# One planned step of a hybrid decoder: both tiles of a group ranked in one stage, the sample's keys loaded at once and its queries spread by TensorE, and the order of all engines planned anew

## The reference, cut to what matters

```python
def block(hc):                                   # 128 tokens
    q = (hc @ w_q).reshape(PEER_CHUNK, PEER_HEADS, 2, PEER_QDIM // 2)
    sc = jnp.einsum('chpd,hpkd->chpk', q, sub_keys)
    s1, i1 = lax.top_k(sc[:, :, 0], 16)
    s2, i2 = lax.top_k(sc[:, :, 1], 16)
    cand = s1[..., :, None] + s2[..., None, :]   # 256 sums a head
    top_s, pos = lax.top_k(cand, 16)             # 16 experts a head, 8 heads
    gate = jax.nn.softmax(top_s, axis=-1)
    act = jax.nn.gelu(einsum('cd,chkd->chk', hc, u[eid]))
    return einsum('chk,chkd->cd', gate * act, v[eid])
```

## Time and profile before

| | us |
|---|---|
| median of 3 executions | 3265.84 (3263.42 to 3266.49) |
| the profiled execution | 3275.52 |
| its span, first to last instruction | 3273.7 |

### The profile page before, as it was taken

The page is one execution under the profiler, slowest core; times in us unless marked ns, Lnnn a source line. Parts: engine busy times, 40 slices in busy tenths (PEclk is TensorE's granted clock), DMA queues, the critical chain, the costliest instruction groups (busy, mean ns, idle before and its releaser), DMA issues.

```text
span 3273.7 us, 38234 instructions
## 1 busy us (share of the span) xinstructions
PE 2734.6 (84%) x9152; PEld 1497.6 (46%) x9152; DVE 2532.3 (77%) x6009; ACT 1827.8 (56%) x5820; POOL 1411.1 (43%) x1044
## 2 busy tenths in 40 slices
PE   7777798889989889989988888579878778878886
PEld 4444354445545545554445545234444334444442
DVE  1288687888788998878888887656989987777775
ACT  1245544678555668755556677344555555555554
POOL 0034232444333444434344454223444456666663
PEclk9888999999999999989999999799999999999998
DMA  9999899999999999999999999988999999999997
GB/s 335 357 387 397 338 392 419 385 377 409 399 391 417 388 398 400 387 365 422 390 361 396 383 395 409 351 300 346 373 372 391 386 403 418 421 420 421 416 418 295
DMA packets 191372, 1262.55 MB, mean 386 GB/s; under 512 B 24849, under 2 KB 32873, under 8 KB 46737
## 3 DMA queue, kind: packets, MB, share of 16 engines
q0 software_dynamic: 149760, 1086.39, 82.5%
q1 hardware_dynamic: 41384, 173.70, 14.2%
HBM read 1251.24 MB, written 43.37 MB: 395 GB/s over the span
## 4 chain that ended last, share of the span: by engine, by line
DMA 28%; DVE 26%; PE 24%; issue 7%; ACT 6%; DVEq 5%; POOL 2%; SPq 1%; ACTq 1%; POOLq 0%
DMA uv_ring<-in_peer_uv,idx 25%; DVE uv_ring L2467 10%; PE acc L1775 9%; DVE accs L2474 5%; PE pS L1530 4%; PE pS L1657 3%; PE pA L1680 2%; POOL uv_ring L1471 1%; ACT bent L2072 1%; ACT wv L2075 1%; ACT diag L1845 1%; DVE onehot L2326 1%; DVE onehot L2329 1%; PE acc L1530 1%; PE pS L1584 1%
## 5 line engine op out<-in xcount | busy, mean ns | idle before, releaser
L1471 POOL DMA_INDIRECT uv_ring<-in_peer_uv,idx x1024 | 1394.5, 1362 | 1816.5 <-PE acc L1775 1352.5
L1775 PE MATMUL acc<-uv_ring,diag 128*128 128x512 f32 x2460 | 1242.9, 638 | 378.5 <-ACT diag L1845 373.3
L2467 DVE SCALAR_TENSOR_TENSOR uv_ring<-uv_ring,hb 128x1024 f32<-128x1024 f32 x1032 | 1240.2, 1221 | 280.0 <-DMA uv_ring<-in_peer_uv,idx 253.5
L1775 PEld LDWEIGHTS acc<-uv_ring,diag 128*128 128x128 f32 x2460 | 454.0, 198 | 943.2 <-ACT diag L1845 525.7
L2068 ACT ACTIVATE cube<-dots 128x1 f32<-128x1 f32 x1032 | 205.8, 199 | 874.5 <-DVE uv_ring L2467 866.2
L2474 DVE SCALAR_TENSOR_TENSOR accs<-uv_ring,wv,accs 128x1024 f32<-128x1024 f32 x409 | 523.4, 1280 | 44.0 <-ACT wv L2075 42.1
L1789 PE MATMUL acc<-maskB,zeros 128*96 128x256 f32 x2162 | 520.8, 384 | 0.0
L1789 PEld LDWEIGHTS acc<-maskB,zeros 128*96 128x96 f32 x2162 | 353.4, 165 | 205.5 <-issue 118.1
L2072 ACT ACTIVATE bent<-dots,cube 128x1 f32<-128x1 f32 x1032 | 399.1, 387 | 74.1 <-issue 2.8
L1845 ACT ACTIVATE diag<-diag,wv 128x128 f32<-128x128 f32 x615 | 247.0, 402 | 50.8 <-issue 1.4
L2075 ACT ACTIVATE wv<-bent,dots 128x1 f32<-128x1 f32 x615 | 238.0, 387 | 43.9 <-issue 1.4
(11 more groups left out here) (279 smaller groups left out, 2225.2 us busy)
## 6 DMA issues: line engine op xcount, KB each, us to landing
wbuf<-in_w_q SPq DMA_DIRECT2D x40, 1024.0 KB
out_dil_s<-in_cache_dil SPq DMA_DIRECT2D x8, 4092.0 KB
wbuf<-in_w_in SPq DMA_DIRECT2D x26, 1024.0 KB
wbuf<-in_w_out SPq DMA_DIRECT2D x20, 1024.0 KB
uv_ring<-in_peer_uv,idx POOLq DMA_INDIRECT x1024
uv_ring<-in_w_in SPq DMA_DIRECT2D x6, 1024.0 KB, 16.3
keysT<-in_keys SPq DMA_DIRECT2D x40, 128.0 KB
T<-in_xT_all SPq DMA_DIRECT2D x8, 512.0 KB, 15.1
```

The source lines that it names most:

```text
L1471: pool.indirect_dma_start(uv_ring[:, entry % RING, :], None, peer_uv, bass.IndirectOffsetOnAxis(rows, 0))\
L1775: m = pe.matmul(acc[0:R, side * 512:(side + 1) * 512], w, uv_ring[:, entry % RING, D + side * 512:D + (side + 1) * 512], start=first, stop ...
L2467: dve.scalar_tensor_tensor(row, row, GELU_C, h, ALU.mult, ALU.mult, accum_out=dots[:, e % RING:e % RING + 1]).then_inc(u_dot, 1)
```

## The change

- A group's two tiles are ranked together: one `r0` and one `r1` for both, so that `top16` runs its five steps over four (or two) parts with one drain ahead of each step. The second tile's sums go into a new buffer, `cand2`, inside `onehot`. The numbers of `max`, `max_index` and `match_replace` are the same as before.
- The sample's queries are no longer spread by DMA. A new stage `sq` on PE (`sample_queries`) multiplies a column of the unit matrix, broadcast, with the eight new query rows, twice 512 columns, into `pS` for even and `pT` for odd tokens; the products read them there. `sq` of token r waits for the products of token r - 2.
- The space of the queries holds keys: each of the 8 tokens has its own buffer `s_kv`, its keys are loaded for all eight right after `sin`'s loads with no wait between, and its values come into the same buffer once its own products are done.
- The planner's numbers: `SPREAD` 1.8 to 2.4, `DMA8` 2.62 to 2.5, the sample's transfers all at `sin` (12.0) and 1.5 for the values of each token, 10 us (`NEW_ROWS`) until the new rows are back, 6 + 3r us until the keys of token r are there and 14 us for values.

```diff
     out = [("sin", 0, 0, 0, 0.0, 2.0)]
+    out += [("sq", 0, 0, 1, 0.9, 0.0)]
     for r in range(NS):
-        out += [("smul", r, 0, 2, 0.0, 2.6), ("smul", r, 1, 0, 0.0, 1.6)]
+        out += [("sq", r + 1, 0, 1, 0.9, 0.0)] if r + 1 < NS else []
+        out += [("smul", r, 0, 1, 0.0, 2.6), ("smul", r, 1, 0, 0.0, 1.6)]
...
-        for t in tiles:
-            out += [("r0", g, h, 0, 0.0, 3.3, t), ("r1", g, h, 0, 0.0, 2.2, t)]
+        out += [("r0", g, h, 0, 0.0, 3.3, tiles), ("r1", g, h, 0, 0.0, 2.2, tiles)]
...
+    if kind in ("r0", "r1"):
+        return (("DVE", {"r0": (3.23, 5.56), "r1": (2.75, 4.43)}[kind][len(s[6]) - 1]),)
...
-SPREAD = 1.8
+SPREAD = 2.4
...
-DMA8 = 2.62
+DMA8 = 2.5
 POOL = 1.4
 FETCH = 12.0
-S_SETS = 4
+NEW_ROWS = 10.0
...
-        if s[0] in ("smul", "spv"):
-            return 1.9
+        if s[0] == "sin":
+            return 12.0
+        if s[0] == "smul" and s[2] == 1:
+            return 1.5
...
+        if BASE[n][0] == "sin" or BASE[n][0] == "sq" and BASE[n][1] < 2:
+            ready += NEW_ROWS
         if BASE[n][0] in ("smul", "spv") and BASE[n][2] == 0:
 
             r = BASE[n][1]
-            if BASE[n][0] == "spv":
-                m = AT["smul", S_SETS + r // 2, 1]
-            else:
-                m = AT["sin", 0, 0] if r < S_SETS else AT["smul", r - S_SETS, 1]
+            m, late = (AT["smul", r, 1], FETCH + 2.0) if BASE[n][0] == "spv" else (AT["sin", 0, 0], 6.0 + 3.0 * r)
             end = self.part_end.get((m, 0))
             if end is None:
                 return None
-            ready = max(ready, end + FETCH)
+            ready = max(ready, end + late)
...
+        cand2 = onehot[:, 1, :, :].rearrange("p a b -> p (a b)")[:, 0:136]
...
-        s_sets = [(KTBf if i < 2 else VBf)[:, 2048 * (i % 2):2048 * (i % 2) + 2048] for i in range(S_SETS)]
-        s_k = [x[:, 0:1024].rearrange("p (s n) -> p s n", s=2) for x in s_sets]
-        s_q = [x[:, 1024:2048] for x in s_sets]
-        s_v = [s_sets[r // 2][:, 1024 * (r % 2):1024 * (r % 2) + 1024].rearrange("p (s n) -> p s n", s=2)
-               for r in range(NS)]
+        s_kv = [(KTBf if r < 4 else VBf)[:, 1024 * (r % 4):1024 * (r % 4) + 1024].rearrange("p (s n) -> p s n", s=2)
+                for r in range(NS)]
...
+        s_kA = [o_all[:, 256 + P * r:384 + P * r] if r < 6 else rest[:, 2752 + P * (r - 6):2880 + P * (r - 6)]
+                for r in range(NS)]
...
+        s_q = [pS, pT]
...
             def sample_keys(r):
-                i = r % S_SETS
-                if r >= S_SETS:
-                    sp.wait_ge(s_mul, r - S_SETS + 1)
-                for dst, src in cache_rows(s_k[i], r, 0):
-                    sp.dma_start(dst, src).then_inc(sk_in[i], 16)
-                sp.dma_start(s_kA[i], cache_swa[r:r + 1, :].rearrange("r (s n) -> (r s) n", n=256)[:, 0:P])\
-                  .then_inc(sk_in[i], 16)
-                sp.dma_start(s_q[i][:, 0:512], zS_scr[r:r + 1, QA:KVA].broadcast_to([P, 512])).then_inc(sk_in[i], 16)
-                sp.dma_start(s_q[i][:, 512:1024], zS_scr[r:r + 1, QB:KB].broadcast_to([P, 512])).then_inc(sk_in[i], 16)
+                for dst, src in cache_rows(s_kv[r], r, 0):
+                    sp.dma_start(dst, src).then_inc(sk_in[r], 16)
+                sp.dma_start(s_kA[r], cache_swa[r:r + 1, :].rearrange("r (s n) -> (r s) n", n=256)[:, 0:P])\
+                  .then_inc(sk_in[r], 16)
...
-                        for r in range(S_SETS):
+                        for r in range(NS):
                             sample_keys(r)
                         sample_masks()
                     elif s[0] == "smul" and s[2] == 1:
-                        if s[1] + S_SETS < NS:
-                            sample_keys(s[1] + S_SETS)
-                        else:
-                            for r in range(2):
-                                sample_values(2 * (s[1] - S_SETS) + r)
+                        sample_values(s[1])
...
-                sp.wait_ge(s_mul, S_SETS + r // 2 + 1)
+                sp.wait_ge(s_mul, r + 1)
...
+            def sample_queries(r):
+
+                if r == 0:
+                    pe.wait_ge(snew_in, 64)
+                    need(pe, a_max, seen["sm"])
+                if r == 1:
+                    need(pe, n_T, seen["ng"])
+                if r > 1:
+                    pe.wait_ge(s_mul, r - 1)
+                for side in range(2):
+                    m = pe.matmul(s_q[r % 2][:, 512 * side:512 * side + 512], idn[0:8, r:r + 1].broadcast_to([8, P]),
+                                  s_newq[:, side, :], start=True, stop=True)
+                m.then_inc(sq_mm, 1)
...
-            def rank_halves(g, h, t):
-                u = PLACE_IN_GROUP[t]
+            def rank_halves(g, h, tiles):
                 dve.wait_ge(k_ev, 16 * g + 2 * h + 2)
                 parts = [(sc[:, (16 * g + 2 * h + half) % SC_SLOTS, u * P:(u + 1) * P], topv[:, u, half, :],
-                          topi[:, u, half, :]) for half in range(2)]
-                m = top16(parts)
-                if t == prompt_of(GROUPS[g])[-1]:
-                    m.then_inc(r_top, 1)
-
-            def rank_sums(u, R):
-
-
-                first, second = topv[0:R, u, 0, :], topv[0:R, u, 1, :]
-                D_()
-                dve.tensor_tensor(cand[0:R, 0:128].rearrange("p (a b) -> p a b", b=8),
-                                  first.unsqueeze(2).broadcast_to([R, TOPK, 8]),
-                                  second[:, 0:8].unsqueeze(1).broadcast_to([R, TOPK, 8]), ALU.add)
-                dve.tensor_scalar(cand[0:R, 128:136], second[:, 8:16], first[:, 0:1], None, ALU.add)
-                top16([(cand[0:R, :], candv[0:R, u, :], candp[0:R, u, :])])
-                return dve.tensor_scalar(gsub[0:R, u, :], candv[0:R, u, :], candv[0:R, u, 0:1], None, ALU.subtract)
+                          topi[:, u, half, :]) for u in range(len(tiles)) for half in range(2)]
+                top16(parts).then_inc(r_top, 1)
+
+            def rank_sums(us, R):
+
+
+                D_()
+                cands = {u: (cand if i == 0 else cand2)[0:R, :] for i, u in enumerate(us)}
+                for u in us:
+                    first, second = topv[0:R, u, 0, :], topv[0:R, u, 1, :]
+                    dve.tensor_tensor(cands[u][:, 0:128].rearrange("p (a b) -> p a b", b=8),
+                                      first.unsqueeze(2).broadcast_to([R, TOPK, 8]),
+                                      second[:, 0:8].unsqueeze(1).broadcast_to([R, TOPK, 8]), ALU.add)
+                    dve.tensor_scalar(cands[u][:, 128:136], second[:, 8:16], first[:, 0:1], None, ALU.add)
+                top16([(cands[u], candv[0:R, u, :], candp[0:R, u, :]) for u in us])
+                for u in us:
+                    m = dve.tensor_scalar(gsub[0:R, u, :], candv[0:R, u, :], candv[0:R, u, 0:1], None, ALU.subtract)
+                return m
...
                 if part == 0:
-                    dve.wait_ge(sk_in[r % S_SETS], 96 * (r // S_SETS + 1))
-                    dot_heads(s_sc[:, 0:2, 8 * r:8 * r + 8], s_k[r % S_SETS].unsqueeze(2),
-                              s_q[r % S_SETS][:, 512:1024].unsqueeze(1).unsqueeze(1).broadcast_to([P, 2, 1, 512]),
+                    dve.wait_ge(sk_in[r], 64)
+                    dve.wait_ge(sq_mm, r + 1)
+                    dot_heads(s_sc[:, 0:2, 8 * r:8 * r + 8], s_kv[r].unsqueeze(2),
+                              s_q[r % 2][:, 512:1024].unsqueeze(1).unsqueeze(1).broadcast_to([P, 2, 1, 512]),
                               1024, P, (2, 1, 2))
```

30 lines of the change are left out of this document (18 added, 12 removed).

## The result

The changed kernel takes 3243.08 us, the median of 5 executions (3241.09 to 3247.91), and the kernel before 3266.49 us beside it (3263.42 to 3274.04). The ratio is 0.9917, 95% interval 0.9895 to 0.9938: 23 us less by the medians, 20 to 34 us by the interval. The profiled execution took 3242.59 us, its span is 3241.0 us. The forecast was 3223 us, so 20 us too good; as a ratio it is 0.987, outside the interval.

What follows compares the result with a forecast made beforehand. The prediction took the DMA gathers as the bound, so gains come from unmoved bytes or a dry ring. Its terms 13 + 17 + 13 = 43 us gave 3232 for the profiled execution, 3223 us as median; range 3190 to 3272.

Steps and rivals of the forecast that it cites:

- Bytes, 13 us: Sample's attention: dropping 16 query spreads, 4.19 MB, saves 13 us, since DMA is nearly full there.
- Rival D: Small transfers slow the gathers beside them, so removing the spreads gains more: 3192 us; chance 0.06.
- The sample's waits, 17 us between 0 and 34: Sample's attention and output projection: fewer waits for loads fill DMA's dry spells, worth at most 34 us; half taken, 17.
- The signs for it: From `sin` to output projection: 370 GB/s or more, no slice under 200, DVE's load waits under 10 us.
- The ranking, 13 us: Ranking two tiles at once saves DVE 1.7 us a head, 41 us in all; 13 counted as time.
- The sign for it: The stretch of the last ranking should run at 385 GB/s or more.
- The order, 0 within 19 us: New lists over the 1850 us ahead of the sample: no effect, bounds 19 us either way.
- Rival C: The new lists lose elsewhere: the 1850 us run at 382 GB/s, 47 us longer, giving 3270 us; chance 0.11.
- The other sign of being wrong: The prediction would be wrong if POOL waits for `idx`, a ranking, after the start.
- The spread on PE, 0: Sample's queries: 16 products take 17 us of PE beside DMA, costing nothing; queries read from PSUM add nothing.
- Rival B: Sample's attention: PE and DVE hold each other up behind late loads, waits of 90 us, 3296 us; chance 0.11.
- Rival A: Only the bytes count; waits move to a crowd of loads and ranking was hidden: 3253 us; chance 0.17.

Runs made afterwards that it cites:

- x2: The changed kernel with its lists kept and the 16 query spreads issued again as loads nobody waits for; 3246.14 us, 0.9932.
- x6: The kernel before with the sample's part of the change alone, old planner numbers, ranking one tile a stage; 3233.70 us, 0.9890.
- x7: The kernel before with the sample's part and the new planner numbers, ranking one tile a stage; 3234.00 us, 0.9893.
- x4: The kernel before, planned with the new SPREAD 2.4 and DMA8 2.5 and otherwise untouched; 3274.47 us, 1.0024.
- x3: The changed kernel planned with the old SPREAD 1.8 and DMA8 2.62; 3257.61 us, 0.9963.
- x5: The kernel before with the merged ranking stages alone, planned anew with the old numbers; 3287.35 us, 1.0054.
- x9: The changed kernel, with its planner expecting a token's values 54 us after its products instead of 14; 3241.37 us, 0.9922.
- x11: x7 with the eight 64 KB loads of near values issued early, right behind the masks; 3234.21 us, 0.9897.
- x10: x7 with every list kept, but both tiles' first two ranking stages done at once at the second tile's place; 3280.45 us, 1.0039.

## Why the prediction was right, and where it was not

The direction and the main reason, the sample's part, held; the sum, 43 us, was 20 too high. That 3243 lies in the range says little, since 3190 to 3272 reached past no change. The sample's part was forecast at 30 us and measured at 30 to 40, and that is in part luck: its two terms were wrong in opposite directions.

- **Bytes, 13 us.** As bytes it is right: 169.50 MB on q1, 1258.25 MB in all, as forecast. As time it is 3 to 5 us (x2), give or take as much again. The step that failed is "DMA is nearly full there, so I take 13 us as saved": the stretch had dry spells, and loads that nobody waits for can lie in them. Rival D priced small loads higher still, and x2 does not show its 25 us. An estimate from the Trainium skill's "DMA: Bandwidth & Descriptors", section "Anatomy of one DMA — SWDGE (gpsimd) path", had 42 us for them. That section is about loads that GpSimd issues, and these went out on SP's queue (q1 in the profile); x2's 3 to 5 us for as many loads of the same size speak against it as a price here.
- **The sample's waits, 17 us between 0 and 34.** With the bytes this was 30 of at most 47. The part as a whole measured 30 to 40 us (x6 against before, x7 against x4, x3 against x5), so the waits alone are 25 to 37. The direction was right, and taking half was too low: the upper value even passes the bound of 34. The signs for it were half wrong: DVE's waits for loads did go, but the stretch ran at 352 GB/s, not 370, and one slice fell to 0. PE took over part of the wait, 16.2 us for values, behind issues of SP that the prediction did not count. x9 and x11 show that such a spell can go without a gain. The dip itself was read too narrowly: beside the slice at 300 GB/s stand 351 and 346, not 380 to 420.
- **The ranking, 13 us.** The saving on DVE was right: 5.47 us for a merged `r0`, (6.24 - 5.47) + (5.30 - 4.52) = 1.55 us a head and the drains in front, where I had 1.7 with them. What failed is "it counts only where DVE holds up DMA", which took the freed time to be idle time of DVE and the plan around it to stay as good. The planner filled the time with 25 weighings (32 us), and the merge cost 9 to 24 us, which the counts of gathers place outside the ranking. This step alone has the wrong sign, and its 13 + 9 = 22 us are as large as the whole error. The sign for it, 385 GB/s in the last ranking, was missed by one. Step by step, the numbers (+8), the sample's part (-40) and the merge (+9) give -23 us, the result; I had 0, -30 and -13. By the other way round the table, merge (+21), sample's part (-30), numbers (-15), the parts are other ones and the sum is the same, so no part has one price.
- **The order, 0 within 19 us.** It lies inside: +8 (x4), 0 (x7 against x6), -15 (the change against x3). Rival C had a rate under 388 GB/s up to `sin` as its sign; it is 395. The other sign of being wrong, POOL waiting for `idx` after the start, did show, once for 2.3 us (5.5 before), and decides nothing. But that the numbers' worth depends on what else is planned I had not seen.
- **The spread on PE, 0.** PE waits under 5 us for DVE at L1731, and DVE 2.5 us for PE at L2406, in all. An operand in PSUM cost nothing here: 1220 ns against 1225 from SBUF. The 62 more cycles that the Trainium skill's "VectorE: DVE Perf Modes", section "The TRN2 errata", gives do not show.
- **Rival B** was priced at 90 us of waits, and decided from 60; there are 16 us of PE for values and 2.5 of DVE for the spreads. The 34 us that it starts from are the worth of the dry spells; the waits listed before add up to 30. **Rival A** (only the bytes, 3253) falls with x2 and x6.

The best kernels of this study are x6 and x7, 3234 us: the sample's part of the change without the merge, by the medians 9 us faster than the whole change.

## What to carry to other kernels

Time saved in one stage of a planned program is spent by the planner before it can be idle: look at what else moved (here the weighings between PE and DVE) before counting it. An experiment that changes a stage's length under lists made for another length measures the misfit as well, so run it in both directions and planned anew. Try each part of a change alone; here the whole was, by the medians, slower than one of its parts. And count where in the program a loss builds up before naming a cause: the merge changed the ranking, and the loss stood elsewhere.

## What was not expected of the hardware

- SP's issues of the same kind of load differ in length by a factor of five and more. The groups of the keys' issues, L1335, and of the values', L1368 (ns minimum, median, maximum):

```profile
L1335 SPq DMA_DIRECT2D KTB<-in_cache_dil x12: 327/432/4392, 2131.7 to 2141.2; - x12
L1335 SPq DMA_DIRECT2D VB<-in_cache_dil x12: 430/1194/5601, 2147.3 to 2171.8; - x12
...
L1368 SPq DMA_DIRECT2D KTB<-in_cache_dil x12: 426/526/3272, 2180.6 to 2193.7; - x12
L1368 SPq DMA_DIRECT2D VB<-in_cache_dil x12: 2107/2704/3436, 2199.8 to 2236.2; - x12
```

  The three issues of a token take 1.4 to 2.2 us for the first three tokens and mostly 7 to 9 from the fourth on, for keys and again for values. The kernel before has such long issues too (up to 4.5 us for one). That loads still under way hold them up is a guess that no run isolates. In the changed kernel they set when the last values can land.
- 16 loads of 256 KB that no engine's work waits for cost 3 to 5 us in a stream of gathers, about a third of their bytes at the stream's rate.
- Fewer busy microseconds on DVE (2490.7 against 2511.1) went with 46 us more time (x10), where only the ranking of the first tiles had moved.
